# Seven block products in place of eight in a feed-forward's first projection

## What is computed

```python
h = h + mx[5] * conv_ffn(modulate(rmsnorm(h, norm2_g[l]), mx[3], mx[4]), w_up[l], conv_w[l], conv_b[l], w_down[l])
```

## Time and profile before

| | us |
|---|---|
| median of 3 runs | 2558.67 |
| lowest and highest | 2556.18, 2562.14 |
| span of the profiled execution | 2559.7 |
| TensorE matmuls busy in it | 2436.9 |
| VectorE busy | 1330.9 |
| ScalarE busy | 840.4 |
| GpSimd busy | 304.3 |
| second layer's up stage (part of the span) | 254.65 |

### The profile page before, as it was taken

One profiled execution on the slowest core, in us unless ns is written; L12 is line 12 of the kernel. 1 busy time (PEld: TensorE's weight loads), 2 busy tenths in 40 slices (PEclk: granted clock), 3 DMA queues, 4 the chain that ended last, 5 costly groups with the idle time before them and its releaser, 6 DMA issues. The chain is left out here.

```text
span 2559.7 us, 35115 instructions
## 1 busy us (share of the span) xinstructions
PE 2436.9 (95%) x14850; PEld 1898.1 (74%) x14850; DVE 1330.9 (52%) x2142; ACT 840.4 (33%) x1346; POOL 304.3 (12%) x246
## 2 busy tenths in 40 slices
PE   6999989999999999999999999998999999999977
PEld 5887568888887888897679999774754579773333
DVE  4323664666667313333757777437657856532223
ACT  3324433333235113324434434224323743420001
POOL 0501420000002000302500000000013020011112
PEclk9999999999999999999999999999999999999999
...
DMA packets 63245, 322.32 MB, mean 126 GB/s; under 512 B 8109, under 2 KB 20397, under 8 KB 31789
## 3 DMA queue, kind: packets, MB, share of 16 engines
...
HBM read 315.82 MB, written 12.58 MB: 128 GB/s over the span
## 5 line engine op out<-in xcount | busy, mean ns | idle before, releaser
L2394 PE MATMUL ps<-xn_rounded,ring_rounded 128*128 128x258 f32 (+2 forms) x2816 | 531.7, 311 | 0.0
L1096 PE MATMUL ps<-work_rounded,ring_rounded 128*128 128x512 f32 (+2 forms) x1952 | 514.7, 352 | 5.2 <-PEq L901 3.6
L1096 PE MATMUL ps<-xn_rounded,ring_rounded 128*128 128x512 f32 (+3 forms) x2176 | 512.2, 347 | 0.0
L2394 PEld LDWEIGHTS ps<-xn_rounded,ring_rounded 128*128 128x128 f32 x2816 | 411.8, 189 | 30.9
L1096 PEld LDWEIGHTS ps<-xn_rounded,ring_rounded 128*128 128x128 f32 (+1 forms) x2176 | 351.7, 190 | 54.1 <-issue 0.2
L1096 PEld LDWEIGHTS ps<-work_rounded,ring_rounded 128*128 128x128 f32 x1952 | 321.9, 190 | 61.2 <-issue 5.0
L1096 PE MATMUL ps<-big_rounded,ring_rounded 128*128 128x512 f32 (+1 forms) x1200 | 319.1, 356 | 11.2 <-DVE big_rounded L996 8.7
L996 DVE TENSOR_TENSOR ring_rounded<-ring,ring_rounded 128x2048 fp32r<-128x2048 f32 (+4 forms) x107 | 191.4, 1789 | 237.0 <-ACT ring_rounded L960 236.8
L2394 PE MATMUL ps<-work_rounded,ring_rounded 128*128 128x256 f32 (+1 forms) x1232 | 278.5, 307 | 1.5 <-PEq L901 1.5
L960 ACT ACTIVATE ring_rounded<-ring 128x2048 fp32r<-128x2048 f32 (+4 forms) x107 | 161.0, 1505 | 311.4 <-PE ps L1096 279.1
L1096 PEld LDWEIGHTS ps<-big_rounded,ring_rounded 128*128 128x128 f32 x1200 | 196.9, 189 | 52.3 <-DVE big_rounded L996 10.5
...
## 6 DMA issues: line engine op xcount, KB each, us to landing
ring<-in_stream SPq DMA_DIRECT2D x141, 1024.0 KB, 4.9
big<-in_experts SPq DMA_DIRECT2D x44, 1024.0 KB, 23.7
...
ring<-in_experts SPq DMA_DIRECT2D x17, 1024.0 KB, 27.3
xn<-in_experts SPq DMA_DIRECT2D x15, 1024.0 KB, 15.2
work<-in_experts SPq DMA_DIRECT2D x15, 1024.0 KB, 16.0
big<-in_first_modulation SPq DMA_DIRECT2D x8, 1024.0 KB, 14.9
...
```

Of the source, the lines that this page charges most:

```text
L1096: mm = pe.matmul(out[:, a - u.first:b - u.first], lhs, rhs, start=j == 0 and n == 0 and not u.onto, stop=j == terms - 1 and n == len(passe ...
L2394: mm = pe.matmul(out[:, a:b], ws[:, k, :], x[k][:, a - base:b - base], start=k == 0 and n == 0, stop=k == KT - 1 and n == 2)
```

## The change

In the second layer only, `ffn_up` is replaced by a class `SevenProducts`. The weights of a strip are seen as 2 x 2 blocks: A11, A12 (first half of the channels, even and odd tiles of D), A21, A22 (second half); the host packs them in this order. The tokens are 2 x 2 blocks too: even and odd tiles of D by the first and the second 256 tokens (B11, B12, B21, B22), each with a column more at either side. The eight block products are replaced by seven, of sums: S1 = A21 + A22, S2 = S1 - A11, S3 = A11 - A21, S4 = A12 - S2 on the weights, T1 = B12 - B11, T2 = B22 - T1, T3 = B22 - B12, T4 = B21 - T2 on the tokens. The products are P1 = A11 B11, P2 = A12 B21, P3 = S4 B22, P4 = A22 T4, P5 = S1 T1, P6 = S2 T2, P7 = S3 T3. Each has 4 tiles x 3 passes = 12 matmuls of 258 columns. They are added up in PSUM: P1, P6, P7, P4 in bank a, and copies and sums between banks for the others.

- GpSimd makes S1 to S4 for each strip (six operations of 128 x 512 in a strip, with the side tap's addition and the gate). S1 to S3 lie in the unused part of h, S4 takes A21's place in the strip.
- ScalarE makes the highs of A11, of S1 and S2 together (1024 columns), of S4 and A22 together (1024), A12 and S3; it copies P1 to bank b (`copy_first`) and P5 to SBUF (`copy_fifth`), makes the centre tap with its bias, the side tap of the second half, and the silu. Its order in round i: side tap (i - 2), the two copies (i), high A11 (i + 1), silu (i - 2), centre (i - 1), highs S1 S2 (i + 1), S4 A22 (i), centre (i - 1), highs A12 and S3 (i + 1).
- VectorE makes the five lows, two sums of a bank and the kept P5 (`make_fourth`, `make_fifth`, 258 columns), two evictions of 514 columns, and three convolution steps of 512 (two of the first half, one of the second).
- P3 and P4 of strip i run third and fourth in the round of strip i + 1, between P5 and P6 of that strip.
- The tokens' blocks, T1 to T4, their splits and the squares are made in the output projection behind the evictions of its tiles; GpSimd adds the squares there. The inverse root is one activation; VectorE's reciprocal goes.
- Before P1 of the first strip, three matmuls of 512 columns on ones are run.
- Of the down projection's tiles 4 are split ahead, not 9; the others after the last product.

```diff
+class SevenProducts:
+        order = []
+        for i in range(FT + 1):
+            order += [("P1", i), ("P5", i)] if i < FT else []
+            order += [("P3", i - 1)] if i >= 1 else []
+            order += [("P4", i - 1)] if i >= 1 else []
+            order += [("P6", i)] if i < FT else []
+            order += [("P2", i), ("P7", i)] if i < FT else []
...
+        if i in (2, 4, 6):
+            self.pair_lows(dve, i // 2 - 1)
+        if i == 6:
+            a = slice(774, 1032)
+            dve.wait_ge(self.squared.sem, self.squared.at(13))
+            dve.tensor_tensor(v["T1"][:, a], v["T3"][:, a], v["B11"][:, a], ALU.subtract).then_inc(self.summed_pair.up(), 1)
+            self.low_a11(dve, 0)
+            self.low_s1_s2(dve, 0)
+            dve.wait_ge(self.high_made.sem, self.high_made.at(self.high_number["even", 3]))
+            for name, low in (("B11", v["B11"][:, a]), ("T1", self.last_t1_low)):
+                dve.tensor_tensor(b.rounded(low), v[name][:, a], b.rounded(self.highs[name][:, a]).bitcast(F32), ALU.subtract)
...
+    def sum_s2(self, pool, n):
+        if n >= 1:
+            pool.wait_ge(self.done.sem, self.after("P6", n - 1))
+        pool.wait_ge(self.sums_made.sem, self.sum_number(n, "S1"))
+        pool.tensor_tensor(self.sums(2, 2), self.sums(0, 2), self.slot(n, 0).rearrange("p (k c) -> p k c", k=2), ALU.subtract).then_inc(self.sums_made.up(), 1)
+    def sum_s3(self, pool, n):
+        self.b.strip(pool, self.first + n)
+        if n >= 2:
+            pool.wait_ge(self.done.sem, self.after("P7", n - 2))
+        pair = lambda part: self.slot(n, part).rearrange("p (k c) -> p k c", k=2)
+        pool.tensor_tensor(self.sums(4 + 2 * (n % 2), 2), pair(0), pair(2), ALU.subtract).then_inc(self.sums_made.up(), 1)
+    def sum_s4(self, pool, n):
+        pool.wait_ge(self.sums_made.sem, self.sum_number(n, "S2"))
+        pair = lambda part: self.slot(n, part).rearrange("p (k c) -> p k c", k=2)
+        pool.tensor_tensor(pair(2), pair(1), self.sums(2, 2), ALU.subtract).then_inc(self.sums_made.up(), 1)
...
+    def add_side(self, pool, i):
+        pool.wait_ge(self.centred.sem, self.centred.at(2 * i + 2))
+        pool.wait_ge(self.side_ready.sem, self.side_ready.at(i + 1))
+        cc = self.cv[:, i % 2, 1, :]
+        pool.tensor_tensor(cc, cc, self.side, ALU.add).then_inc(self.gated.up(), 1)
...
+    def gpsimd(self, pool):
+        self.add_square(pool, KT - 1)
+        self.sum_s1(pool, 1)
+        self.sum_s2(pool, 1)
+        for i in range(FT + 1):
+            if i + 1 < FT:
+                self.sum_s4(pool, i + 1)
+            if i + 2 < FT:
+                self.sum_s3(pool, i + 2)
+            if 0 <= i - 2:
+                self.gate(pool, i - 2)
+            if i + 2 < FT:
+                self.sum_s1(pool, i + 2)
+            if 0 <= i - 1 < FT - 1:
+                self.add_side(pool, i - 1)
+            if i + 2 < FT:
+                self.sum_s2(pool, i + 2)
...
+    def product(self, pe, name, i):
+        weight, source, bank, start = {"P1": ("A11", "B11", "a", True), "P5": ("S1", "T1", "e", True), "P6": ("S2", "T2", "a", False),
+                                       "P2": ("A12", "B21", "b", False), "P7": ("S3", "T3", "a", False), "P3": ("S4", "B22", "d", False),
+                                       "P4": ("A22", "T4", "a", False)}[name]
+        high_w, low_w = self.weight_parts(weight, i)
+        out = self.bank_of(bank, i)
+        for j in range(4):
+            if i == 0 and j == 3 and name in ("P6", "P2", "P7", "P3", "P4"):
+                pieces = {"P6": "T2", "P2": "three", "P7": "three", "P3": "three", "P4": "T4"}
+                pe.wait_ge(self.low_made.sem, self.low_made.at(self.low_number[pieces[name], 3]))
+            low_x, high_x = self.source_parts(source, j)
+            pe.matmul(out, high_w(j), low_x, start=start and j == 0, stop=False, skip_group_check=True)
+            pe.matmul(out, high_w(j), high_x, start=False, stop=False, skip_group_check=True)
+            mm = pe.matmul(out, low_w(j), high_x, start=False, stop=j == 3, skip_group_check=True)
+        mm.then_inc(self.done.up(), 1)
...
+    def tensor(self, pe):
+        b = self.b
+        for n in (2, 3, 6):
+            pe.matmul(b.bank(n), b.ones, b.base[:, 0:512], start=True, stop=True)
+        for i in range(FT + 1):
+            if i < FT:
+                if i >= 2:
+                    pe.wait_ge(self.scaled.sem, self.scaled.at(2 * (i - 2) + 2))
+                if i >= 1:
+                    pe.wait_ge(self.low_made.sem, self.low_made.at(self.low_number["a11", i]))
+                self.product(pe, "P1", i)
+                if i >= 1:
+                    pe.wait_ge(self.low_made.sem, self.low_made.at(self.low_number["s1_s2", i]))
+                self.product(pe, "P5", i)
+            if i >= 1:
+                pe.wait_ge(self.partial_summed.sem, self.partial_summed.at(2 * i - 1))
+                pe.wait_ge(self.low_made.sem, self.low_made.at(self.low_number["s4_a22", i - 1]))
+                self.product(pe, "P3", i - 1)
+            if i >= 1:
+                pe.wait_ge(self.partial_summed.sem, self.partial_summed.at(2 * i))
+                self.product(pe, "P4", i - 1)
+                b.strips_freed(1)
+            if i < FT:
+                pe.wait_ge(self.first_copied.sem, self.first_copied.at(i + 1))
+                self.product(pe, "P6", i)
+                pe.wait_ge(self.low_made.sem, self.low_made.at(self.low_number["a12", i]))
+                self.product(pe, "P2", i)
+                pe.wait_ge(self.partial_summed.sem, self.partial_summed.at(2 * i + 1))
+                pe.wait_ge(self.low_made.sem, self.low_made.at(self.low_number["s3", i]))
+                self.product(pe, "P7", i)
...
+            if 0 <= i - 2:
+                self.weigh_side(act, i - 2)
+            if 1 <= i < FT:
+                self.copy_first(act, i)
+                self.copy_fifth(act, i)
+            if i + 1 < FT:
+                self.high_a11(act, i + 1)
+            if 0 <= i - 2:
+                self.silu(act, i - 2)
+            if 0 <= i - 1 < FT - 1:
+                self.bias(act, i - 1, 0)
+                self.centre(act, i - 1, 0).then_inc(self.centred.up(), 1)
+            if i + 1 < FT:
+                self.high_s1_s2(act, i + 1)
+            if i < FT:
+                self.high_s4_a22(act, i)
+            if 0 <= i - 1 < FT - 1:
+                self.bias(act, i - 1, 1)
...
+    def low_a11(self, dve, n):
+        b = self.b
+        dve.wait_ge(self.high_made.sem, self.high_made.at(self.high_number["a11", n]))
+        dve.wait_ge(self.sums_made.sem, self.sum_number(n, "S2"))
+        dve.wait_ge(self.sums_made.sem, self.sum_number(n, "S3"))
+        self.low_of(dve, self.slot(n, 0), b.rounded(self.slot(n, 0)), self.high_place("A11"))
...
+    def make_fourth(self, dve, i):
+        dve.wait_ge(self.done.sem, self.after("P6", i))
+        dve.wait_ge(self.fifth_copied.sem, self.fifth_copied.at(i + 1))
+        if i == 1:
+            dve.wait_ge(self.rooted.sem, self.rooted.at(1))
+        dve.tensor_tensor(self.bank_of("d", i), self.bank_of("a", i), self.fifth_kept[i % 2], ALU.add).then_inc(self.partial_summed.up(), 1)
+    def make_fifth(self, dve, i):
+        dve.wait_ge(self.done.sem, self.after("P7", i))
+        dve.tensor_tensor(self.bank_of("e", i), self.bank_of("a", i), self.fifth_kept[i % 2], ALU.add).then_inc(self.partial_summed.up(), 1)
...
+        for i in range(FT + 1):
+            if 1 <= i < FT:
+                self.low_s1_s2(dve, i)
+            if i >= 1:
+                self.low_s4_a22(dve, i - 1)
+                self.make_fifth(dve, i - 1)
+            if 0 <= i - 2:
+                self.convolve_first(dve, i - 2, 0)
+            if 1 <= i < FT:
+                self.low_s3(dve, i)
+                self.low_a12(dve, i)
+            if 0 <= i - 2:
+                self.convolve_first(dve, i - 2, 1)
+            if i == 1:
+                dve.wait_ge(self.rooted.sem, self.rooted.at(1))
+            if i >= 1:
+                self.evict(dve, i - 1, 0)
+            if 0 <= i - 2:
+                self.convolve_second(dve, i - 2)
+            if i < FT:
+                self.make_fourth(dve, i)
+            if i + 1 < FT:
+                self.low_a11(dve, i + 1)
+            if i >= 1:
+                self.evict(dve, i - 1, 1)
...
+        def release_last(act, k):
+            if k == tiles_ahead:
+                act.wait_ge(self.done.sem, seven.all_done)
+                act.wait_ge(seven.gated.sem, seven.after_gate(FT - 4))
+            if k in (7, 8, 9):
+                seven.tap_last(act, 0, k - 7)
+            if k in (11, 12, 13):
+                seven.tap_last(act, 1, k - 11)
+            if k == 16:
+                seven.silu_last(act)
+            if k in (FT - 3, FT - 2):
+                act.wait_ge(seven.gated.sem, seven.after_gate(k))
+            if k == FT - 1:
```

(15 more changed lines are left out.)

442 lines of the change are left out of this document (421 added, 21 removed).

## The result

| | before | after |
|---|---|---|
| median, us | 2559.3 (4 runs, 2556.18 to 2562.14) | 2636.49 (4 runs, 2627.39 to 2637.35) |
| span of the profiled execution | 2559.7 | 2635.5 |
| up stage: first product to the end of the last | 254.65 | 317.1 |
| granted clock, mean of the span | 0.991 | 0.981 |

The change makes the kernel slower: ratio 1.0288, interval 1.0268 to 1.0308. The sign was forecast, the size was not: +77 us against +17.8, outside the range.

A forecast was written before the change was run, and what follows sets the result against it. The prediction took TensorE to bound the stage before, and one queue of GpSimd's and VectorE's two-operand work after: -30.4 + 42.9 + 1.0 + 2.8 + 1.5 = +17.8 us on 2558.7, so 2576 us, range 2562 to 2590.

The forecast's parts named there:

- TensorE's products: Up stage: 84 matmuls a strip for 96, 10.08 us a strip for 11.52, 31.7 us less over 22 strips.
- The three matmuls of ones: Ahead of the first strip's P1: about 0.43 us each, 1.3 us in all.
- The mechanism: Up stage: two-operand work of GpSimd and VectorE goes one after the other as one queue, 1.69 us a pair.
- the ordinary round: Up stage: the queue makes a strip take 12.4 us, against 10.08 for TensorE alone.
- The tiles split ahead: Down projection's first unit has 4 tiles split ahead instead of 9; ScalarE must split 18 tiles on the way out.
- the way out: From the up stage into the down projection: 1.5 us more with the same clock fall; -3 or +4 otherwise.
- The stands forecast here are of that size: TensorE's waits in the strips: about 1 us each, like the experts' stage's 1.4 us, where the clock holds 1.00.
- the 18.5 rounds: Up stage: about 18.5 rounds have all six GpSimd operations, 18.5 x (12.4 - 10.08) = 42.9 us lost; light strips go at TensorE's pace.
- VectorE's PSUM work (2.2 us) lies beside GpSimd and is not in it: Up stage: VectorE's 2.2 us of PSUM work per strip runs beside GpSimd and adds nothing to the 12.4 us queue.
- The way in: Output projection into the up stage: last eviction 3.8 us late, near 1339.4, with 1.0 given back: +2.8 us.
- TensorE keeps the stage: First rival: GpSimd's turns fall into VectorE's PSUM work and waits; 10.08 us a strip, -25.1 us, 2534 us; chance 0.26.
- VectorE's lag adds to the queue: Second rival: one turn lost per strip, 13.5 us a strip, 2597 us, or 2605 with clock falls; chance 0.14.

The follow-up runs named there:

- 3: On the kernel of 1, nearly all of GpSimd's two-operand work in the up stage replaced by constants or 8-column operations: 2535.44 us.
- 4: On the kernel of 1, a measuring piece ahead of the first layer: seven cases of six operations on VectorE, GpSimd or both; 2682.91 us in one run.
- 6: On the kernel of 5, the gate of rounds 2 to 22 made by VectorE behind the fourth's sum instead of GpSimd: 2603.76 us.
- 1: On the changed kernel, VectorE's low parts of the tiles split ahead, and of the down strip, made one round later: 2615.84 us.
- 11: On the kernel of 1, fourth's sum directly behind the third tap, ahead of the eviction; ScalarE's highs of S1, S2 ahead of bias and centre tap: 2610.6 us.
- 5: On the kernel of 1, ScalarE's high parts of a strip pair put ahead of assembling and squaring on the way in: 2618.82 us.

## Why the prediction missed

**TensorE's products, right.** 10.09 us for a strip against 10.08, shown by 3. The three matmuls of ones were priced too low, see below.

**The mechanism, right.** GpSimd's and VectorE's two-operand work is one queue (1.67 us a pair, 1.69 forecast), and it sets the ordinary round. Shown by 3, 4 and 6 together. GpSimd's operations take 1.5 to 2.3 us, VectorE's lows 1.78, as the prediction said they would.

**The tiles split ahead, the step that failed.** The prediction counted the split of 4 tiles in the way out and gave its place in the stage no price and no wait. It costs 21 us with the strip's in round 21, shown by 1: four times 3.4 us and once 3.0 of VectorE's stand, and what follows, TensorE's stand of 3.3 us and 6.8 us at 0.50. How the remaining 4 us divide between the two was not tried. "The stands forecast here are of that size", 1.4 us, was said without a look at which wait of VectorE's comes last in each kind of round.

**The ordinary round, a term too small.** 12.4 forecast, 13.33 measured in 1; with the 18.5 rounds that is 17 us. The step: "VectorE's PSUM work (2.2 us) lies beside GpSimd and is not in it". Work beside it can only be where GpSimd has something to do just then. VectorE's PSUM work is 1.9 us by its starts; the eviction at 1421.56 and the fifth's sum had GpSimd beside them, 0.94 us, the fourth's sum and the second eviction did not, since S3's place wasn't free yet. From below: 7.9 of VectorE's own + 6 x 1.07 is 14.3; 0.94 beside gives 13.4, the measured round. All of it beside would be 12.5, the forecast. The same count gives 13.6 for the 13.66 measured over strips 5 to 20 of 1, and 12.8 for the 13.09 of 11, where only the order was changed. The rest of the stage's excess is 1.5 rounds that I took as light and that ran at 13.3 (5 us), and some 7 in the first strip and the tail, which I can't place.

**The way in and out.** First product 1346.24; with the forecast's +2.8 and the 1.3 for the matmuls of ones it would be 1341.75: 4.5 more. The last eviction is at 1341.14 for 1339.4, as VectorE waits 3.10 us for highs that I had ready 1.6 earlier. Then the three matmuls of ones took 3.8 us for 1.3:

```profile
1342.42 4.38 PE L806 MATMUL ps<-base 128*128 128x512 f32 x6 [6.48 <-PEq L1553]
```

Three instructions are six entries here. The four of the earlier trace rows that I divided 1.88 us by were two instructions (`output_projection` has `waiting=(1, 2)`), so the price is 0.86 each and not 0.43, 2.6 us in all, and the forecast should have read +19.1. The other 1.2 us are, as an estimate, the lower clock behind TensorE's stand of 6.5 us (0.50 from 1338.8 to 1345.6 us), a term I had not. That GpSimd's work has its part in the way in is shown by 3 and 5; the clock's part alone was not tried. The way out is +4.7 for +1.5. Its first unit takes as long as before (21.4 us for 21.6): the longest stand there is 1.2 us for 2.3, and the clock holds 1.00 where its mean was 0.84, so the forecast's same fall did not come. All of the 4.7 lies in small differences along the 950 us behind it, where the granted clock is 0.98 for 0.99. From the stage's end on, the experiments vary between 969 and 976 us. That remains open.

Together 4.5 + 50.3 (stage 317.1 for 266.8, which is 254.65 - 31.7 + 42.9 + 1.0) + 3.2 = 58.0, the distance of +75.8 from +17.8.

**The rivals.** "TensorE keeps the stage" fails by 3.2 us a round. "VectorE's lag adds to the queue" has nearly the right round, 13.5, by another mechanism: no turn was lost, the overlap was. Its 2597 to 2605 us were still short by over 31, as it had no price for the tiles split ahead either. Falls of the clock came, and more often than now and then, but those of the ordinary rounds cost nothing (1 and 4).
